# The out projection on VectorE: residual sum ahead of the turned rows' copy, experts chosen four tiles at a time, idle products near the end

## The reference

```python
mix = jnp.concatenate([y_a, y_b.reshape(bt, s, W_B)], axis=-1) @ w_out
x = layer_norm(DEEPNORM_ALPHA * x + mix, ln1_g, ln1_b)
...
scores = jax.nn.sigmoid((xt @ w_router).astype(f32))
biased = scores + router_bias.astype(f32)
grouped = biased.reshape(-1, N_EXPERT_GROUPS, EXPERTS_PER_GROUP)
group_score = lax.top_k(grouped, TOP_K)[0].sum(-1)
sel_group = jnp.argmax(group_score, axis=-1)
...
_, top_idx = lax.top_k(masked, TOP_K)
gates = top_s / top_s.sum(-1, keepdims=True)
```

## Time and profile before

| | |
|---|---|
| median of 3 runs | 1327.16 us (1325.23 to 1327.24) |
| the profiled execution's span | 1326.7 us |
| busy: PE, DVE, ACT, POOL | 1197.5, 929.0, 526.3, 479.1 us |
| out projection | about 500 to 769 us of the span |
| DMA over the whole span | 290.05 MB, 219 GB/s |
| DMA from 530 to 760 us | 57.52 MB, 250 GB/s |

### The profile page before, as it was taken

One profiled execution on the slowest core, in us unless ns is written; L12 is line 12 of the kernel. 1 busy time (PEld: TensorE's weight loads), 2 busy tenths in 40 slices (PEclk: granted clock), 3 DMA queues, 4 the chain that ended last, 5 costly groups with the idle time before them and its releaser, 6 DMA issues. The chain is left out here.

```text
span 1326.7 us, 24018 instructions
## 1 busy us (share of the span) xinstructions
PE 1197.5 (90%) x7133; PEld 1021.8 (77%) x7134; DVE 929.0 (70%) x2023; ACT 526.3 (40%) x847; POOL 479.1 (36%) x552
## 2 busy tenths in 40 slices
PE   7999999999878889999998778999999999999920
PEld 7997999878767656888787677888887888888820
DVE  3463997468866655568877577777777777777776
ACT  4131110111003353232332125666666666666564
POOL 4008860110030004323222032545454554546457
PEclk9999999999989999999989788999999999999975
DMA  9599684576255332577877665899999789755495
GB/s 255 179 318 281 213 255 120 143 263 223 81 142 153 92 134 71 173 263 252 271 281 264 230 254 206 276 270 288 309 284 302 235 235 314 211 126 102 101 361 214
DMA packets 142834, 290.05 MB, mean 219 GB/s; under 512 B 54632, under 2 KB 71608, under 8 KB 131472
## 3 DMA queue, kind: packets, MB, share of 16 engines
q1 hardware_dynamic: 126320, 231.99, 50.7%
q0 software_dynamic: 15408, 55.12, 17.7%
q10 hardware_dynamic: 1040, 2.10, 0.5%
HBM read 177.90 MB, written 111.13 MB: 218 GB/s over the span
## 5 line engine op out<-in xcount | busy, mean ns | idle before, releaser
L2267 DVE TENSOR_TENSOR wgu<-w_raw,wgu (+1 forms) x192 | 229.7, 1219 | 85.1 <-ACT wgu L2378 83.6
L2532 PE MATMUL p_gu<-wgu,xg_high 128*128 x768 | 246.4, 402 | 8.3 <-DVE xg_low L2260 4.5
L2378 ACT CAST wgu<-w_raw x188 | 192.7, 1052 | 57.1 <-issue 54.0
L2532 PEld LDWEIGHTS p_gu<-wgu,xg_high 128*128 128x128 f32 x768 | 141.6, 191 | 42.3 <-issue 15.1
L2532 PE MATMUL p_gu<-wgu,xg_low 128*128 x384 | 151.7, 395 | 0.0
L2141 POOL TENSOR_TENSOR spare_e<-nothing 128x1 f32<-128x1 f32 x48 | 46.5, 968 | 219.6 <-DVE yo L2286 219.6
L2142 POOL DMA_INDIRECT acc_rows<-yo,si x48 | 112.3, 2340 | 8.7 <-issue 8.7
L1899 PE MATMUL p_out<-w_out_high,mixt_high 128*128 128x512 f32 x256 | 103.5, 404 | 0.0
L1899 PE MATMUL p_out<-w_out_high,mixt_low 128*128 128x512 f32 x256 | 101.6, 397 | 0.0
L1899 PE MATMUL p_out<-w_out_low,mixt_high 128*128 128x512 f32 x256 | 101.5, 396 | 0.0
L2532 PEld LDWEIGHTS p_gu<-wgu,xg_low 128*128 128x128 f32 x384 | 72.9, 190 | 15.8
(11 more groups left out here) (478 smaller groups left out, 2946.4 us busy)
## 6 DMA issues: line engine op xcount, KB each, us to landing
w_raw<-in_w_gate SPq DMA_DIRECT2D x16, 1024.0 KB
w_raw<-in_w_up SPq DMA_DIRECT2D x16, 1024.0 KB
wd_high<-w_down_high SPq DMA_DIRECT2D x16, 1024.0 KB
wd_low<-w_down_low SPq DMA_DIRECT2D x16, 1024.0 KB
ya_u<-in_w_down SPq DMA_DIRECT2D x46, 256.0 KB, 4.1
w_down_low<-ya_r SPq DMA_DIRECT2D x46, 256.0 KB, 6.7
acc_rows<-ax SPq DMA_DIRECT2D x18, 512.0 KB, 8.0
w_down_high<-yb_r SPq DMA_DIRECT2D x34, 256.0 KB, 7.0
```

The source lines that it names most:

```text
L2267: low = tt(wgu[:, slot, 1, at], raw[:, slot, at], wgu[:, slot, 0, at].bitcast(F32), ALU.subtract)
L2378: nc.scalar.copy(wgu[:, slot, 0, at], raw[:, slot, at]).then_inc(hi_set, 1)
L2532: mm = t.matmul(pg[b][:, :, :], x[:, b, k, :], w[h][:, k], start=(k == 0 and x is xh and h == 0), stop=(k == KD - 1 and x is xl))
```

## The change

Four edits. On DVE `norm` is cut in two: `residual` (the wait for the product and the sum that frees the banks) and the rest. The order for a tile is now residual, copy of the turned rows of the tile before, rest of the normalisation, units. The experts are chosen for four tiles at a time, after tiles 6, 10 and 14, and for the last five at the end; the scratch tiles grow for that from 4 to 5. On PE 24 idle products of 128 columns go ahead of `turn(16)`; they wait for the residual sum of tile 15, whose bank they write.

```diff
@@
+            SEL = 5
@@
-                def norm(c, b, first, half, n=P):
-
+                def residual(c, b, half, n=P):
                     dve.wait_ge(z_in[b], (half + 1) * 16)
                     dve.wait_ge(o_prod, c + 1)
                     for m in range(2):
                         cols = slice(m * SUP, (m + 1) * SUP)
                         v.scalar_tensor_tensor(z[0:n, b, cols], z[0:n, b, cols], ALPHA, po[b][m][0:n, :], ALU.mult,
                                                ALU.add).then_inc(z_set, 1)
+
+                def norm(c, b, first, half, n=P):
                     dve.wait_ge(z_set, c * 2 + 2)
@@
                 dve.wait_ge(row_in, 32)
+                residual(0, 0, 0, NS)
                 norm(0, 0, True, 0, NS)
+                residual(1, 1, 0)
+                turn(0, 0, True, NS)
                 norm(1, 1, True, 0)
-                turn(0, 0, True, NS)
-                for b in range(2):
-                    norm(2 + b, b, False, 1)
-                    turn(1 + b, 1 - b, b == 0)
-                units(2)
-                dve.wait_ge(sel_set, 7)
-                dve.wait_ge(rb_in, 16)
-                for i in range(2, CH // 2 - 1):
-                    for b in range(2):
-                        norm(i * 2 + b, b, False, i)
-                        turn(i * 2 + b - 1, (b + 1) % 2)
-                        units(i * 2 + b - 1)
-                    select(i * 2 - 4, 2, i * 2 - 1)
-                for b in range(2):
-                    norm(CH - 2 + b, b, False, CH // 2 - 1)
-                    turn(CH - 3 + b, 1 - b)
-                    units(CH - 3 + b)
-                select(CH - 6, 3, CH - 2)
+                CHOICES = {6: 0, 10: 4, 14: 8}
+                for c in range(2, CH):
+                    residual(c, c % 2, c // 2)
+                    turn(c - 1, 1 - c % 2, c == 2)
+                    norm(c, c % 2, False, c // 2)
+                    units(c - 1)
+                    if c == 4:
+                        dve.wait_ge(sel_set, 7)
+                        dve.wait_ge(rb_in, 16)
+                    if c in CHOICES:
+                        select(CHOICES[c], 4, c - 1)
                 turn(CH - 1, 1)
+                residual(CH, 0, CH // 2)
                 norm(CH, 0, False, CH // 2)
                 turn(CH, 0)
-                select(CH - 3, 4, CH + 1, True)
+                select(CH - 4, SEL, CH + 1, True)
@@
                 router(CH - 2, 0, False)
                 router(CH - 1, 1, False)
+                pe.wait_ge(z_set, CH * 2)
+                for _ in range(24):
+                    t.matmul(po[1][0][:, 0:P], ident[:], ident[:], start=True, stop=True)
                 turn(CH, 0, False)
                 router(CH, 0, False)
```

More of the change, by code:

```diff
@@ L1538, in hybrid_step @@
             tmp_s = Place(nc, us_at)
+            SEL = 5
             w4, w16_, rb = (sb(n, [P, k], where=tmp_s) for n, k in (("w4", EG), ("w16r", E), ("rb", E)))
[L1540 to L1543, removed]
+            s_bi, s_m1, s_mid = (sb(n, [P, SEL, E], where=tmp_s) for n in ("s_bi", "s_m1", "s_mid"))
+            s_p6 = sb("s_p6", [P, SEL, EG, 6], where=tmp_s)
+            s_gs, s_gq = sb("s_gs", [P, SEL, EG], where=tmp_s), sb("s_gq", [P, SEL, EG], where=tmp_s)
+            s_red, s_s1, s_s2 = (sb(n, [P, SEL], where=tmp_s) for n in ("s_red", "s_s1", "s_s2"))
             live = sb("live", [P, 1], where=tmp_s)
```

## The result

The changed kernel takes 1331.44 us (median of 9 runs, 1326.89 to 1335.2), the kernel before 1327.16 in the same comparison (9 runs, 1323.53 to 1328.25): a ratio of 1.0033, 95% interval [1.0019, 1.0046]. It is 4.3 us slower where I had forecast 1.6 us faster. The profiled execution's span is 1332.0 us, 5.3 more than before.

What follows compares the result with a forecast made beforehand. The DMA loop was taken to pace the second half of the stage, which ends in a chain across engines. Steps traced to the last choice's end gave 766.7 against 768.33, so 1327.2 - 1.6 = 1325.6 us; range 1321.8 to 1330.0.

Steps and rivals of the forecast that it cites:

- The DMA loop: SP's cycle of loads and waits for stores to land sets when units are ready; step 13 at 720.4, step 14 at 737.1.
- the choice's place: Choice for four (7.2 us) behind step 13's units delays tile 15's `x1` to 736.1; TensorE waits 7 us or more.
- The start of the loop: SP's loads of step 6, no longer behind a choice, bring the loop 1.5 us earlier, bounds 0 to 3.1.
- what TensorE had lost: Since 724.89: 4.2 us waiting, at least 1.7 slow scores, 1.8 slow products; without these it reaches tile 15 by 728.6.
- The idle products: Ahead of turning tile 16: 5.5 us at full clock, holding it 2.9 us, returning 0.9 and 1.7: about nothing.
- my first rival: Clock falls before the idle products: 8.6 instead of 5.5 us, tile 16 waits 3.1 longer, 1328.7 us; chance 0.17.
- All later work follows the barrier behind it: Everything after the stage's closing barrier was taken to shift by exactly as much as the stage's end.
- my 766.7: Forecast end of the last choice, and so of the stage, in us; 768.33 before, 1.6 us less.
- The other rivals: Slower loop, 1329.0 us, chance 0.10; more from the loop, 1321.5, 0.15; choice moves nothing on the path, 1327.2, 0.13.
- The price of a choice that meets GpSimd: Choice ahead of tile 15 beside POOL's low parts: counted nothing; a meeting on this path would end the stage at 769.3.
- My 1.3 us for each meeting: By the exclusive lock on shared ports, each meeting of a VectorE choice with a POOL low part costs 1.3 us.

## Why the prediction was wrong

**The DMA loop and the choice's place: right in mechanism, within a us in size.** Loads of step 13 at 713.17 (712.7 in my count), 15.6 ahead of those of step 14; the choice for four behind the units; TensorE held 9.25 us at turning tile 15 (7 or more), at 737.08 (736.1); slow products behind it, 8.8 us from the turning to the scores (8.8 to 9.9); the scores of tiles 14 and 15 from 745.89 (745.5); `x1` of tile 16 at 752.3 (751.6). The start of the loop gave 0.6 us instead of 1.5: my upper bound of 3.1 was a misreading, SP's own waits allowed 1.6, and the landing moved too. In the count of what TensorE had lost I took 1.7 for slow scores from another row; those behind 724.89 took 3.16 us in the trace, 1.3 more than 1.85, which changes nothing of "7 us or more". Up to here I am 0.7 us off.

**The idle products: the step that failed.** I wrote "48 records in 5.5 us at the full clock, to 754.5" and "about nothing in sum". They took 7.9 us, to 758.6, and held tile 16 for 6.3 us, not 2.9. What they give back, 2.6 us, was sized right (0.9 and 1.7). Net 3.7 us where I had 0.3. This was my first rival, at a chance of 0.17; its argument was the right one, and mine against it ("the scores of every tile pass at the full clock") was a misreading: one tile's scores of 1.85 us stand between products of 512 columns, while here two tiles' stood in a row. The second ran at 2.77 already. The run with the idle products ahead of the scores shows it: 5.4 us there, and the slow clock 4.1 us after the scores' start. The rival's own price, 1328.7 us, was still 2.7 too low, by what follows.

**"All later work follows the barrier behind it, and I let it shift by as much as that end shifts": failed as well.** The counting product is 2.5 us later, the experts 5.2. Of the other 2.7, 1.1 goes with the 24 instructions' being in TensorE's program: the cast of the first weights comes 8.4 to 8.9 us after the counting product in all seven profiles that hold them, wherever they stand, and 7.5 to 7.7 in the nine with 8 or none. On ScalarE the work for the lists stands behind that cast, and the list products start 7.9 us after it in fifteen profiles, 8.1 in the sixteenth. So the later cast makes the wait ahead of them longer, 3.3 instead of 2.3 us, and behind waits of 2.76 or more the list products took 9.43 (or 10.91) in six profiles of seven, behind waits of up to 2.4 never. That is the other 1.6.

**Sum.** From my 766.7 for the stage's end: 0.7 by which `x1` of tile 16 was later, and 3.4 for the idle products (6.3 of holding instead of 2.9; 1.3 of it because the scores ahead of them were slower than I took), is 770.8, where the last choice ends (770.60 + 0.24). That is 2.5 above before's 768.33; with the 2.7 behind the barrier it is 5.2 of the profiled 5.3. That the sum closes so well is partly luck: the rest of the expert stage lasted 526.5 and 526.4 us in these two executions, and varied by 5.8 over all. The timed difference is 4.3.

**The rest.** Without idle products the kernel takes 0.9993 of before [0.998, 1.0007], -1.0 us; my sum without them gives -1.9. The interval holds that and no change alike, so the time agrees with the forecast and doesn't prove it; the rows above do more for it. The other rivals didn't come: the loop's steps were neither slower nor quicker, and TensorE did wait for the choice. The price of a choice that meets GpSimd wasn't tested: GpSimd did nothing from 714.3 to 734.0, and the choice took 7.2 us, as I had counted. My 1.3 us for each meeting was too high in any case: before, the instructions at 649.83 and 650.91 took 0.9 and 1.0 us more than their like, and each ended just behind GpSimd's.

**What stays open:** by what path 24 more TensorE instructions go with a landing of the first weights, or a cast behind it, that is 1.1 us later. The issue of the loads isn't late: SP issues the first of these loads 0.19 us ahead of the counting product before and after (769.46, 771.98). The transfers of instructions in the DMA table are 39 packets instead of 38 on one queue in six of the seven, but not in the seventh, so this doesn't settle it. Open too is why order and choices are each slightly slower alone, and why the clock stayed up behind a wait of 3.17 us and not behind one of 2.76.

## What to carry to other kernels

Idle products for the clock paid nowhere here, neither ahead of the tile that the end waits for nor in TensorE's own wait behind it. Before adding any, look at what TensorE does just ahead of them; where that is small products, price them at the lower clock, and set what they hold against what they return (here 6.3 us against 2.6). A batch of small work on an engine belongs into a wait that this engine already has: the same choice for four tiles, moved across one call of `units`, was worth some 4 to 6 us. And when an end is made of a chain, look at what the next stage does with the time it gets: in one run quicker products there only made a longer wait, and slower products behind it.

## What the runs showed of the hardware

- TensorE's clock fell during uninterrupted work, when that work was score products of 16 columns: full at 750.62, at the lower level by 754.74, with 0.36 us of idle time in between; in the changed kernel full at 745.89 and at the lower level from 749.0. Idle products of 128 columns kept it (745.26 to 750.62) or brought it back (at 755.7, begun at 750.72).
- The same list products take 7.80, 9.43 or 10.91 us: with a granted clock of 1.00 throughout, with one that falls in their second us (0.67 from 790 to 795), or at 0.50 from their start. A wait of 3.17 us was once followed by 7.80 and one of 2.76 by 9.43, so the length of the wait alone doesn't decide. The Trainium skill (TensorE: Matmul & The Clock Gate, "What's actually happening") warns that the number of slow products varies from run to run of one kernel; the two rows would fit that, but they come from two kernels with one profile each, so no run here shows it.
- With 24 more instructions on TensorE, executed in the stage before, the first weight cast of the next stage came 8.4 to 8.9 us behind its first product in seven profiles of seven, and 7.5 to 7.7 in the nine with 8 or none. The cause isn't known.
